# Moving the context rows of a second block into the expert stage of the first

## What is computed

```python
def expert_block(args):
    xblk, e = args
    h = jax.nn.silu(xblk @ w_gate[e]) * (xblk @ w_up[e])
    return h @ w_down[e]

x_lat, x_ctx = x, ctx
for l in range(DEPTH_2):                       # 2
    last = l == DEPTH_2 - 1
    h_c = modulate(rms_norm(x_ctx, g_attn[l]), csh1, csc1)
    gl_c, mq_c, mk_c, mv_c, nq_c, nk_c, nv_c = mixer_proj(h_c, *proj_w)
    ...
    y_mla = blocked_attention(mq, jnp.concatenate([mk_c, mk], axis=1),
                              jnp.concatenate([mv_c, mv], axis=1)).reshape(b_, s_, MLA_HEADS * MLA_V)
    y_na = neighborhood_attention(nq, nk, nv, nk_c, nv_c, rpb[l])
    ...
    if not last:
        y_mla_c = dense_attention(mq_c, mk_c, mv_c).reshape(b_, l_, MLA_HEADS * MLA_V)
        y_na_c = dense_attention(nq_c, nk_c, nv_c).reshape(b_, l_, NA_HEADS * NA_DIM)
        x_ctx = x_ctx + cgt1 * gated_merge(gl_c, y_mla_c, y_na_c, w_mla_o[l], w_na_o[l], w_out[l])
        x_ctx = x_ctx + cgt2 * squared_relu_mlp(h2_c, w_ff1[l], w_ff2[l])
```

## Time and profile before

| | us |
|---|---|
| median of 3 runs | 4670.97 (4670.17 to 4675.53) |
| the profiled execution, its own time | 4672.83 |
| span of that execution | 4671.1 |
| TensorE busy | 4024.0 (86%) |
| VectorE, ScalarE, GpSimd busy | 1110.8, 693.2, 172.6 |
| moved by DMA | 507.78 MB, mean 109 GB/s |

### The profile page before, as it was taken

How to read it: one execution, slowest core, us unless ns; L and a number is a source line. 1 busy time by engine, 2 the same in 40 slices (tenths; PEclk the granted TensorE clock), 3 DMA queues, 4 the chain that set the end, 5 groups by cost and what they waited for, 6 DMA issues and landing times. The chain is left out here.

```text
span 4671.1 us, 36718 instructions
## 1 busy us (share of the span) xinstructions
PE 4024.0 (86%) x14700; PEld 2133.1 (46%) x14700; DVE 1110.8 (24%) x2450; ACT 693.2 (15%) x1619; POOL 172.6 (4%) x374
## 2 busy tenths in 40 slices
PE   8986876997577772979989989999979798999999
PEld 3653854444222220645454445554436445444443
DVE  0147523112100003156160131000011525021100
ACT  0213111000000001136150010100012324011000
POOL 1010000000100001030000000000000300000000
PEclk9987886998799896889999999999989899999999
DMA  7532012223699994010101031121121101122221
GB/s 271 186 113 99 1 40 102 87 72 119 226 397 395 398 384 154 25 61 1 45 19 40 32 126 36 54 81 54 44 84 49 37 28 37 54 99 82 72 97 47
DMA packets 232255, 507.78 MB, mean 109 GB/s; under 512 B 19652, under 2 KB 28916, under 8 KB 231944
## 3 DMA queue, kind: packets, MB, share of 16 engines
q1 hardware_dynamic: 218904, 472.52, 27.8%
q0 software_dynamic: 7184, 23.91, 1.4%
q10 hardware_dynamic: 6000, 9.01, 0.5%
HBM read 473.16 MB, written 32.26 MB: 108 GB/s over the span
## 5 line engine op out<-in xcount | busy, mean ns | idle before, releaser
L337 PE MATMUL ps<-ring,layer_hT 128*128 128x512 f32 (+2 forms) x2176 | 822.3, 538 | 8.9 <-PEq L272 8.9
L337 PEld LDWEIGHTS ps<-ring,layer_hT 128*128 128x128 f32 x2176 | 409.0, 197 | 411.7 <-issue 402.2
L2913 PE MATMUL ps<-ring,mlp_hidden 128*128 128x512 f32 x1280 | 549.8, 592 | 2.8 <-PEq L272 2.8
L337 PE MATMUL ps<-layer_hT,ring 128*128 128x512 f32 (+1 forms) x1536 | 550.5, 521 | 1.9 <-PEq L272 1.9
L337 PEld LDWEIGHTS ps<-layer_hT,ring 128*128 128x128 f32 x1536 | 291.7, 190 | 259.8 <-issue 246.6
L2913 PEld LDWEIGHTS ps<-ring,mlp_hidden 128*128 128x128 f32 x1280 | 243.0, 190 | 309.1 <-issue 309.1
L1999 PE MATMUL ps<-ring,moe_xgT 128*64 128x512 f32 x512 | 256.9, 661 | 91.3 <-issue 90.4
L1999 PEld LDWEIGHTS ps<-ring,moe_xgT 128*64 128x64 f32 x512 | 74.9, 152 | 257.4 <-issue 257.3
L337 PE MATMUL ps<-ring,mixers_xT 128*128 128x512 f32 (+2 forms) x448 | 157.0, 505 | 6.9 <-DVE ab_qk L331 5.9
L1999 PE MATMUL ps<-deep_ring_more,moe_hT 128*64 128x512 f32 x256 | 124.2, 642 | 39.9 <-DMA deep_ring_more<-in_e_down 39.1
L2840 DVE TENSOR_TENSOR ps<-ps,mlp_gt 128x512 f32<-128x512 f32 x20 | 14.0, 700 | 541.9 <-PE ps L2913 541.9
(11 more groups left out here) (611 smaller groups left out, 4433.4 us busy)
## 6 DMA issues: line engine op xcount, KB each, us to landing
deep_ring_more<-in_e_down SPq DMA_DIRECT2D x33, 2048.0 KB, 20.5
ring<-in_e_gate SPq DMA_DIRECT2D x32, 2048.0 KB, 25.0
ring<-in_w_ff SPq DMA_DIRECT2D x32, 2048.0 KB, 8.1
ring<-in_w_in SPq DMA_DIRECT2D x26, 2048.0 KB, 10.4
ring<-in_w_ada SPq DMA_DIRECT2D x18, 2048.0 KB, 10.6
ring<-in_e_up SPq DMA_DIRECT2D x16, 2048.0 KB, 21.2
mixers_ring_more<-in_e_up SPq DMA_DIRECT2D x16, 2048.0 KB, 19.9
mixers_ring_more<-in_w_ada SPq DMA_DIRECT2D x6, 2048.0 KB, 10.4
```

Source lines behind the costliest of these rows:

```text
L337: last = pe.matmul(out, lhsT, rhs, start=(j == 0), stop=(j == len(pairs) - 1))
L2913: last_ = pe.matmul(M.ps[:, bank_of(half, t), :], hidden[:, k * DK + j, t * P:(t + 1) * P], w[:, j, :], start=(k == 0 and j == 0), stop=(k ...
```

## The change

1. The 256 context rows leave both layers. `context_sections` writes their whole computation (layer 0, and layer 1's keys and values) as a list of 37 sections of groups, one for each weight tile that they read; `context_tiles` puts these 37 tiles (loaded a second time for the context alone) into the ring's list. `deep_order` and `by_slot` spread the sections over the 32 slots of the expert stage (two per pair: after `gate`, `up`, `turn_x`; and after the `down` groups), by a table of costs `CTX_COSTS`.
2. Context keys and values of each layer go to DRAM from there (8 stores, ScalarE's queue), and each layer loads them (4 more loads on SyncE, `small`). The layers treat 4 tiles of rows everywhere.
3. `DEEP` is 5 instead of 6. The context works in SBUF of the first block's finished tiles (`xT`, `o0T` to `o3T`, `ada_rows`) and in new buffers.
4. Expert weights are laid out with rows 8p to 8p+7 on partition p (one run of 16 KB each, also for `down`); the transposes of the gathered rows and of h read every 8th and every 4th column to match. `spare_experts` does the same.
5. `rwkv_inverse`: level 0 starts from the identity, so its first product and its transposed update fall away, and the last level's untransposed half too.
6. `rms_groups` can share buffers for its squares; the low-rank queries get a buffer of their own (`cqT`).

```diff
-DEEP = 6
+DEEP = 5
@@ experts
+        order, places = deep_order()
+        index, at = {}, t0
+        for name, n in order:
+            index[name, n] = at
+            at += 1 if name == "ctx" else 2
+        sc = st.ctx.enter_context(Stage(nc, "ctx"))
+        sections, load_ctx = context_sections(M, sc, lambda i: index["ctx", i])
+        filler = by_slot(sections, places, 2 * pairs)
...
-                    k = 4 * half + x
-                    last = pe_.transpose(bank[:, x * P:(x + 1) * P], xg[:, n % 2, k * P:(k + 1) * P], M.ident[:, :])
+                    rows = xg[:, n % 2, :].rearrange("p (q k) -> p k q", k=DK)
+                    last = pe_.transpose(bank[:, x * P:(x + 1) * P], rows[:, 4 * half + x, :], M.ident[:, :])
...
-            gs += [flip, *downs]
+            gs += filler[2 * n] + [flip, *downs] + filler[2 * n + 1]
...
-        products(M, "moe_main", gs, tiles=6 * pairs, extra={"gpsimd": gathers})
+        products(M, "moe_main", gs, tiles=at - t0, extra={"sync": load_ctx, "gpsimd": gathers})
@@ new
+CTX_COSTS = [10, 16, 8, 10, 13, 32, 16, 16, 40] + [12, 8, 12] * 2 + [16, 22] + [16] * 16 + [14, 14, 16, 20]
+def deep_order():
+    pairs, total = NE // 2, sum(CTX_COSTS)
+    places = [2 * pairs * sum(CTX_COSTS[:i]) // total for i in range(len(CTX_COSTS))]
+    order = []
+    for n in range(pairs):
+        order += [("gate", n), ("up", n)] + [("ctx", i) for i, p in enumerate(places) if p == 2 * n]
+        order += [("down", n)] + [("ctx", i) for i, p in enumerate(places) if p == 2 * n + 1]
+    return order, places
+def context_sections(M, st, tile):
...
+    first, hT_made = normed("rms0", 0, 0, 0, wait=lambda t: sig[f"x{t}"])
+    low, low_work, ups, keys, kT, v = latent_rows(0, (tile(0), tile(3)), hT_made)
+    sections.append([gained] + first + low + low_work)
...
+    sections += [turned + uq[0], uq[1] + k_work + q_work + k_turned + saves + q_turned + mixed]
...
@@ program
+            for x in range(2):
+                tiles.append((w[0, 2 * n + x].rearrange("(p k) n -> p k n", p=P), w.shape[2] // P, width))
@@ latent_attention
+                sp.dma_start(kT[:, :, T:T + CTX], M.ctx_k[l].rearrange("p (h n) -> p h n", h=MH)).then_inc(s, 16)
+                sp.dma_start(v[:, TT:TA, :], M.ctx_v[l].rearrange("p (t n) -> p t n", t=TC)).then_inc(s, 16)
-            kv = row_groups(M, t0, 0, KV_LORA, hT, lambda t: ckv[:, t, :], rows=TA * P)
+            kv = row_groups(M, t0, 0, KV_LORA, hT, lambda t: ckv[:, t, :])
@@ second_block
-            L = Layer(TT if last else TA)
-            hT = st.sb("hT", [P, DK, TA * P])
+            L = Layer(M.mod[l])
+            hT = st.sb("hT", [P, DK, T])
@@ rwkv_inverse, TensorE
-            for lv in range(6):
+            for q in range(4):
+                pe.wait_ge(sig["quarters"], q + 1)
+                for x in range(4):
+                    last = pe.matmul(bank(4 + q)[:, x, :], xT[:, 4 * q + x, :], M.ident[:, :], start=True, stop=True)
+                last.then_inc(sig["zxz"], 1)
+            for lv in range(1, 6):
...
+                    if lv == 5:
+                        continue
```

More of the change, by code:

```diff
@@ L277, in _ @@
             W.load(sp)
+            if extra and "late" in extra:
+                extra["late"](sp)
         @block.tensor
@@ L307, in mover @@
                     g.evac(eng, None, link).then_inc(moved[on], 1)
+            for g in groups:
+                if g.dma and g.on == on:
+                    eng.wait_ge(g.landed, 16)
         @block.vector
@@ L1690, in merge @@
         t0 = M.weights.taken
[L1691 to L1706, removed]
-                        if n == 0:
-                            return eng.tensor_tensor(merged[:, t, cols], sg[:, slot, :], bank, ALU.mult)
-                        link(eng.tensor_tensor(tmp[:, slot, :], sg[:, slot, :], bank, ALU.mult))
-                        return eng.tensor_tensor(merged[:, t, cols], merged[:, t, cols], tmp[:, slot, :],
-                                                 ALU.add)
-                    out = group(
-                        lambda pe, bank, wb=wb, rows=rows, n=n, cols=cols: matmuls(
-                            pe, bank, [(oT[n][:, k, rows], wb[:, k, cols]) for k in range(wb.shape[1])]),
-                        ev, "v", t0 + 3 * n + 1, after=(gate,))
-                    gs += [gate, out]
-                    used.append(out)
-        products(M, name + "_p", gs, tiles=3 * len(oT))
+        parts = merge_groups(M, lambda i: t0 + i, xT, oT, merged, sg, tmp, tiles)
+        products(M, name + "_p", [g for part in parts for g in part], tiles=3 * len(oT))
 def layer_norm(M, name, x, tiles, gain, bias):
@@ L2284, in second_tiles, with __init__, rms_groups @@
     return tiles
-def rms_groups(M, st, name, x, tiles, heads, d, gain=None, rope=None, made=None, load=None, out=None):
-    sq = st.sb(f"{name}_sq", [P, 2, heads * d])
+class Squares:
+    def __init__(self, bufs):
+        self.bufs, self.last = bufs, ()
+def rms_groups(M, st, name, x, tiles, heads, d, gain=None, rope=None, made=None, load=None, out=None, share=None):
+    if share is None:
+        own = st.sb(f"{name}_sq", [P, 2, heads * d])
+        share = Squares([own[:, i, :] for i in range(2)])
+    sq, before = [b[:, 0:heads * d] for b in share.bufs], share.last
     ss = st.sb(f"{name}_ss", [P, tiles, heads])
@@ L2340, in rms_groups @@
     for t in range(tiles):
-        after = list(made[t]) if made else []
+        after = (list(made[t]) if made else []) + list(before if t < 2 else ())
         if t >= 2:
@@ L2353, in rms_groups @@
                                after=(scales[t], *turns[-1:])))
+    share.last = tuple((sums if heads > 1 else squares)[-2:])
     work = []
@@ new lines, in by_slot @@
+def by_slot(sections, places, slots):
+    out = [[] for _ in range(slots)]
+    for i, section in enumerate(sections):
+        end = places[i + 1] if i + 1 < len(places) else slots - 1
+        held = max([j for j, g in enumerate(section) if g.tile is not None], default=-1) + 1
+        out[places[i]] += section[:held]
+        tail, n = section[held:], end - places[i] + 1
+        for j in range(n):
+            out[places[i] + j] += tail[len(tail) * j // n:len(tail) * (j + 1) // n]
+    return out
```

611 lines of the change are left out of this document (431 added, 180 removed).

## The result

The changed kernel takes **4604.6 us** (median of 4 runs, 4602.9 to 4606.7) against 4673.25 for the kernel before in the same job: a ratio of 0.9849, 95% interval 0.983 to 0.9867. It is faster by 1.5%. The forecast was 4598 in a range of 4520 to 4665.

What follows compares the result with a forecast made beforehand. DMA bounds the experts, TensorE the layers; the change turns the expert stage TensorE-bound. 4672.8 − 538.7 (layers, between, entry) − 8.7 (inverse) + 474.4 (expert stage and end) = 4599.8, or 4598 us against the median; range 4520 to 4665.

Steps and rivals of the forecast that it cites:

- Layers: Four row tiles instead of six: layer 0 −476.3 us, layer 1 −48.4, between the layers −9.
- 902 of work: Expert stage: TensorE work before any waits, 358 us of its own plus 544 received from the context.
- sum about 90: Expert stage: TensorE's exposed waits from norms, attention starts, flips of h, others, and 12 us of half clock.
- 207 us of exposure: Slower rival: the context's vector work doesn't overlap in the expert stage, 207 us in place of 90, total 4715; chance 0.10.
- the second case: Larger-gain rival: well interleaved list, exposures of 30 us in the expert stage, strided reads free, total 4519; chance 0.12.
- Strides: Expert stage: transposes reading every 8th and 4th column cost 19 us more, between 0 and 40.
- Contiguous weights: Expert weights in longer runs cost nothing: packets already 2 KB and more, rate near 396, slack hides any change.
- the cover: Expert stage: DMA needs 765 us, some 245 below the forecast stage, so changes of rate are hidden.
- Ring of five: Expert stage's weight ring: five slots for six costed at nothing, given 245 us of DMA slack.
- The rival of a DMA bound in single pairs: Expert stage: DMA still binds in the eight leanest pairs, some 30 us, total about 4630; chance 0.08.
- Inverse: Triangular inverse: last level's half 3.74 us, level 0 about −5; together −8.7, between −4 and −13.
- The stage's end: End of the expert stage: 3 us for landings of the stores of keys and values.

Runs made afterwards that it cites:

- e2: Kernel before, with only contiguous expert weights and the strided transposes to match (ring of six, no context moved): 4645.05 us, ratio 0.9937.
- e4: Changed kernel with all 37 context sections behind the last pair of experts, not woven: 4732.3 us, ratio 1.0127 to the kernel before.
- e5: Changed kernel with the transposes of h two context groups further forward in each pair: 4575.5 us, ratio 0.9782 to the kernel before.
- e6: Changed kernel with norms' vector work kept in its slot, their transposes started in the next, layer 0's context-key norm moved up: 4573.6 us, ratio 0.9779.
- e8: Changed kernel with four ring slots in place of five in the expert stage: 4653.9 us, ratio 0.9949 to the kernel before.

## Why the prediction was right, and where it wasn't

- **The bound.** Right. DMA bound the stage before (e2: 7% more rate, 7% less stage), TensorE's idle time under it was the gain (e4: 128 us), and the changed stage is bound by TensorE.
- **Layers.** Right: −474.9, −43.8, −8.3 for −476.3, −48.4, −9. The layers' two matmul counts are equal now (3296 each). The 3 us between them are within what layers of the same instructions differ by in all runs here (1103 to 1112). The longer ones show TensorE busy for 1037 to 1040 us at a mean clock of 0.97, the shorter ones 1031 to 1035 at 0.98; what sets the clock there stays open. (The listed parts of the 48.4 add up to 48.6.)
- **Context in the stage.** Right to 1%: 902 of work and 12 for the half clock make 914, and TensorE was busy for 923.4. The two parts of the 902 can't be told apart in the woven stage; in e4, by itself, the context kept TensorE busy for 565.3 us at a clock of 0.93 where 544 were forecast. The idle time of 76.4 stands for the 78 that are left of "sum about 90". By kind the idle time was: flips 23.2 (19 forecast), head norms 18.9 for layer 0 and 1 (22), row norms 11.2 (17), attention 8.1 (8), the rest 15 (10). Neither 207 us of exposure nor 30 came about; e5 and e6 then showed that the second case was to be had with another order.
- **Strides.** Wrong: "The load grows by 0.73; of a transposition of 0.14 us that is 0.1 ... 19 us". The load grew by 0.34 to 0.48 and lay beside the matmuls. A transposition of rows took 0.15 us (19.4/128) in place of the 0.24 forecast, and the cost was 1.3 us, near the lower bound. The step that failed took the load as the transposition's pace. This is more than the 11 us by which the stage came out shorter than forecast.
- **Contiguous weights.** The sum's zero was right, its first reason wrong. "The rate is near 396" was taken as the ceiling; it rose to 416 and would have given 30 us to the kernel before. The second reason, the cover, held.
- **Ring of five.** The zero can't be far off (3.6 us of waits on gate tiles), but the reason "245 us of slack hides any change" was wrong as a rule: one slot less, and the stage grew by 54 us with the same bytes to move. The rival of a DMA bound in single pairs, which named the depth, did not come about with five slots and did with four.
- **Inverse.** Under half the term. The step "eight copies of 0.43 no longer stand ahead" counted TensorE and VectorE work, and not what the new idle time does to the clock behind it. Of the 6 us that the start of the experts missed, a further 2.7 arose ahead of the inverse, where the kernels are alike: the branch's first product starts at 428.2 for 425.5. Over all traces here it starts between these two, so this is the spread of executions.
- **The stage's end.** Mis-sized: 3 forecast, 12.3 measured. "The stores wait for nothing on TensorE" was true and beside the point. ScalarE holds the block open until they land, the store of y stands behind them (8.0 us), and the gather behind that takes 4.2 longer, as in every kernel with contiguous weights in that block.

So the total was 7 us off, and that it was so little is partly luck: the strides were put 18 us too high, while the stage's remaining TensorE work came out 8 dearer, its end 9 and the inverse 6.

## What to carry to other kernels

Where a stage is bound by DMA, another stage's TensorE work can be put inside its idle time, even if weights are loaded twice: here 536 us left the second block (layers, the time between them, the entry), and the expert stage with the block behind it grew by 472. What decided was the order, since the same work behind the stage lost 1.3%. Once woven, the profile's list of waits is the list of what to do next: put some other group between each pair of producer and consumer (here two edits of a few lines gave another 1.3%), and look again at what was free before, such as the layout of the weights. Slack in mean bandwidth wasn't cover for a shallower ring (e8): count the slots that a burst needs. And before a difference of 10 us between two traces is given a cause, compare stretches with the same instructions, which here differed by up to 8.

## What I hadn't expected of the hardware

- Runs of 16 KB moved 416 GB/s over the stage where runs of 2 KB moved 387, with one core running.
- A small gather issued beside three loads of such runs took 4 to 5 us longer than beside the same loads in short runs (11.2 to 11.8 us for 6.4 to 7.0, fourteen kernels); whether the run length or the faster issue does it is open.
- A weight load with a stride of 8 or 4 columns took 50 to 67 ns longer and cost the matmul stream under 10 ns each.
- Behind an idle of 6.05 us a group of 3.8 us took 6.6, at a granted clock of 0.55, so a chain that is shortened on one engine can hand back half of it.
